# A two-layer decoder trunk on one core: POOL takes the candidate adds and half of the up stage's splits, the lookup goes by ranks, the row products read their common row in PSUM, ten chunks stand beside the search

## The chip, the core and the metric

The kernel runs on one core of a Trainium2 chip. A core has five engines that run their own instruction queues in order: TensorE (PE), VectorE (DVE), ScalarE (ACT), GpSimd (POOL) and SyncE (SP), which here only issues DMAs. They wait for each other through semaphores. The metric is the device time of one execution in microseconds.

## The reference

Two layers, each a mixer of three kinds of attention and then a PEER expert network; at the end a norm. The change touches the PEER part alone, for 512 tokens of width 1024:

```python
q = (xc @ w_q).reshape(PEER_CHUNK, PEER_HEADS, 2, PEER_DK_HALF)     # 8 heads, 2 x 128
s1 = jnp.einsum('thd,nd->thn', q[:, :, 0], k1f)                      # 128 sub-keys each
s2 = jnp.einsum('thd,nd->thn', q[:, :, 1], k2f)
v1, i1 = lax.top_k(s1, 16)
v2, i2 = lax.top_k(s2, 16)
cand = v1[..., :, None] + v2[..., None, :]                           # 16 x 16 pairs
cand_id = i1[..., :, None] * 128 + i2[..., None, :]
top_s, top_pos = lax.top_k(cand, 16)
ids = jnp.take_along_axis(cand_id, top_pos, axis=-1)
g = jax.nn.softmax(top_s, axis=-1)
act = jnp.einsum('thkd,td->thk', u[ids], xc)
w = g * jax.nn.gelu(act, approximate=False)
y = jnp.einsum('thk,thkd->td', w, v[ids])
```

u and v are tables of 16384 experts x 1024, float32.

## The kernel before

All weights come through one stream of chunks of 128 x 2048 float32 (1 MB), two slots deep. For each chunk SyncE loads `raw[s]`, ACT writes `hi[s]`, the chunk rounded to fp32r (`split_hi`, L501), and DVE or POOL writes `lo[s] = raw - hi` (`split_lo`, DVE L836, POOL L462). PE multiplies each pair by three matmuls (`product`, L1325 to L1327: hi x hi, lo x hi, hi x lo) and so keeps float32's precision. SyncE loads a slot again when `lo_done` says that it has been split.

The PEER part of a layer goes through these stages:

- Query stage, 8 chunks, one per head: queries, then the scores of its sub-keys; ACT puts these into `scores`.
- Search, on DVE, beside the query stage and the first chunks of the up stage. `top16` finds the best 16 of 128 keys for 4 token tiles x 2 halves (`vals`, `top_i`), two adds (L1106, L1108) form 112 candidate pairs per token (4 x 16 and 12 x 4), and a second `top16` finds the best 16 pairs. After eight heads comes the lookup: the place of each pair is taken apart into two ranks (L1117 to L1130), and for a = 1 to 15 one compare (L1150) marks where a rank is a and one predicated copy (L1153) puts the a-th key's number there, each over 1024 elements. Then the softmax is finished (L1161 to L1167), and `idx_t`, `g_t`, `ids` are ready.
- Up stage, 64 chunks: `experts` computes act for 352 tokens and all experts, 48 matmuls a chunk, in two halves i = 0 and 1 into banks 0 and 1; ACT evacuates them by gelu (L703, L706) and stores them to HBM. The first FIND_STEPS = 14 chunks run beside the search. Chunks 2 to 8 are split in halves by POOL (HALVED, L480), the next by DVE in between the lookup's operations, at a in LOW_HALF_AT.
- After chunk 13 PE transposes the indices and gates into banks 2 to 4 (L1611 to L1613). It waits there for `idx_done` and `g_done` of DVE. Then 30 gate steps follow, each with one chunk and three groups of four tokens, for which DVE and ACT make one-hots and PE multiplies them (L1623) into banks 4 to 7, which ACT evacuates (L749) to HBM. 20 chunks without groups follow: the tail.
- The other 160 (32 "extra" tokens, spread over partitions, and 128 of tile 3) go by gathered rows: POOL fetches 128 rows of u with one indirect DMA into one of NR = 7 slots (L490), DVE multiplies them by the token's row (`x_e` for the first 32 operations, L1202, `x_row` for the rest, L1204) and sums. 32 + 128 such products stand in the gate steps and the tail.
- Down stage, 64 chunks of v: gates and activations come back from HBM, are multiplied (L1238), split (L791, L1243), and `weighted` runs 48 matmuls per chunk into all eight banks in the order V_BLOCKS. The rows of v are fetched and accumulated beside it (L1212, L1215).

Every engine's order is written out by hand in the code. DVE and ACT split one chunk ahead of PE (`ahead`).

```python
for i in range(2):
    experts(st // 2, st % 2, i, halved=st if st in HALVED else None)
for tt in IDX_AT.get(st, ()):
    pe.wait_ge(idx_done, l * NT + tt + 1)
    pe.wait_ge(g_done, l + 1)
```

## Time and profile before

| | us |
|---|---|
| median of 3 runs | 3315.04 |
| lowest and highest | 3309.36, 3315.66 |
| the profiled execution | 3316.17 |
| its span, first to last instruction | 3314.4 |
| PE busy in the span | 3269.3 |
| DVE busy | 2610.5 |
| ACT busy | 1554.9 |
| POOL busy | 1087.6 |

The mean granted clock of TensorE is 0.998 of full speed. In the timelines a row is a start, a duration, the engine, the line of the kernel, the operation with its output and inputs, and in square brackets the engine's idle time before it and what ended that. Matmuls overlap, so their pace is read from start to start. In layer 0 the query stage begins at 484 us, the up stage at 586, the gate steps at 695, their last chunk ends at 1004, the down stage begins at 1158 and ends at 1650.

### The profile page before, as it was taken

What the parts mean: (1) busy time and instruction counts of PE and PEld (TensorE: products, weight loads), DVE (VectorE), ACT (ScalarE), POOL (GpSimd) and SP (SyncE); (2) the same over time, 40 slices, a digit from 0 to 9 for tenths busy, and PEclk for the clock granted to TensorE, in tenths of its full rate; (3) what the DMA queues carried; (4) which work ended last, traced back from release to release, by engine and by line L of the source; (5) the groups of instructions that cost most, each with busy time, mean ns of one, the idle gap of its engine ahead of it and who ended that gap; (6) DMA issues with size and microseconds to landing.
All of it is one profiled execution on the core that took longest, in us unless ns stands there. A gap on an engine that the chain in (4) does not pass through costs nothing. (4 is left out here: it accounts for less than half of the span.)

```text
span 3314.4 us, 55810 instructions
## 1 busy us (share of the span) xinstructions
PE 3269.3 (99%) x19734; PEld 3039.2 (92%) x19734; DVE 2610.5 (79%) x4992; ACT 1554.9 (47%) x2368; POOL 1087.6 (33%) x711
## 2 busy tenths in 40 slices
PE   8999999999999999999999999999999999999998
PEld 7767878999999999999987678789999999999998
DVE  6555448999997899999855644399999978999897
ACT  5554332467774333333355543334677733333333
POOL 1000003423335555555300000134333345555552
PEclk9999999999999999999999999999999999999999
DMA  4113322479999999999721133224899999999996
GB/s 146 62 52 115 140 104 81 171 286 383 379 383 389 420 403 411 403 409 410 284 90 64 42 124 140 103 82 176 310 379 382 378 404 416 402 409 407 404 405 251
DMA packets 230935, 894.83 MB, mean 270 GB/s; under 512 B 22784, under 2 KB 67984, under 8 KB 182912
## 3 DMA queue, kind: packets, MB, share of 16 engines
q1 hardware_dynamic: 116944, 465.34, 36.7%
q0 software_dynamic: 93008, 337.91, 26.1%
q10 hardware_dynamic: 20832, 89.74, 6.7%
q8 instruction: 72, 1.18, 0.1%
q14 instruction: 79, 0.65, 0.1%
HBM read 801.42 MB, written 91.49 MB: 269 GB/s over the span
## 5 line engine op out<-in xcount | busy, mean ns | idle before, releaser
L836 DVE TENSOR_TENSOR lo<-raw,hi 128x2048 fp32r<-128x2048 f32 (+1 forms) x320 | 728.9, 2278 | 287.4 <-ACT hi L501 284.9
L1325 PE MATMUL bank<-xT_hi,hi 128*128 128x352 f32 (+1 forms) x2688 | 928.7, 346 | 1.9 <-DVE xT_lo L886 1.7
L1326 PE MATMUL bank<-xT_lo,hi 128*128 128x352 f32 (+1 forms) x2688 | 911.5, 339 | 0.0
L1327 PE MATMUL bank<-xT_hi,lo 128*128 128x352 f32 (+1 forms) x2688 | 911.3, 339 | 0.0
L501 ACT ACTIVATE hi<-raw 128x2048 fp32r<-128x2048 f32 (+1 forms) x338 | 643.9, 1905 | 375.9 <-PE bank L1327 338.2
L1325 PE MATMUL bank<-w_hi,hi 128*128 128x352 f32 x2048 | 661.1, 323 | 0.5 <-DVE w_lo L1243 0.5
L1327 PE MATMUL bank<-w_hi,lo 128*128 128x352 f32 x2048 | 661.5, 323 | 0.0
L1326 PE MATMUL bank<-w_lo,hi 128*128 128x352 f32 x2048 | 658.1, 321 | 0.0
L1325 PEld LDWEIGHTS bank<-xT_hi,hi 128*128 128x128 f32 x2688 | 506.5, 188 | 32.3 <-issue 5.6
L490 POOL DMA_INDIRECT rows<-in_v_rows,ids x256 | 415.8, 1624 | 350.5 <-DVE h L1215 276.1
L1327 PEld LDWEIGHTS bank<-xT_hi,lo 128*128 128x128 f32 x2688 | 505.7, 188 | 26.0
L1326 PEld LDWEIGHTS bank<-xT_lo,hi 128*128 128x128 f32 x2688 | 507.2, 189 | 23.1
L490 POOL DMA_INDIRECT rows<-in_u_rows,ids x256 | 325.3, 1271 | 394.0 <-DVE act_row L1204 309.8
L1327 PEld LDWEIGHTS bank<-w_hi,lo 128*128 128x128 f32 x2048 | 386.7, 189 | 0.0
L1325 PEld LDWEIGHTS bank<-w_hi,hi 128*128 128x128 f32 x2048 | 384.4, 188 | 1.6 <-issue 1.0
L1326 PEld LDWEIGHTS bank<-w_lo,hi 128*128 128x128 f32 x2048 | 385.8, 188 | 0.0
L1215 DVE SCALAR_TENSOR_TENSOR h<-rows,w_row,h 128x1024 f32<-128x1024 f32 x256 | 327.6, 1280 | 7.3 <-DVE h L1215 1.4
L1204 DVE CUSTOM_DVE_ANT_0 rows<-rows,x_row 128x1024 f32<-128x1024 f32 x256 | 301.1, 1220 | 12.6 <-DMA rows<-in_u_rows,ids 12.6
L791 ACT ACTIVATE w_hi<-act_in 128x704 fp32r<-128x704 f32 x120 | 95.3, 794 | 392.2 <-DVE act_in L1238 392.2
L706 ACT ACTIVATE act_s<-bank 128x352 f32<-128x352 f32 x124 | 57.6, 465 | 278.3 <-PE bank L1327 278.3
L1262 DVE TENSOR_SCALAR onehot<-iota_sb,idx1T,gT 128x128 f32<-128x128 f32 x704 | 185.8, 356 | 1.0 <-ACT gT L738 1.0
L1623 PE MATMUL bank<-onehot 128*128 128x128 f32 x1408 | 176.0, 275 | 0.0
(227 smaller groups left out, 4254.1 us busy)
## 6 DMA issues: line engine op xcount, KB each, us to landing
raw<-in_stream SPq DMA_DIRECT2D x352, 1024.0 KB, 6.6
gate_d<-gate_s ACTq DMA_DIRECT2D x22, 2048.0 KB, 11.9
act_d<-act_s ACTq DMA_DIRECT2D x120, 352.0 KB, 6.4
act_in<-act_d SPq DMA_DIRECT2D x120, 352.0 KB, 7.0
gate_in<-gate_d SPq DMA_DIRECT2D x96, 384.0 KB, 9.6
gate_in<-gate_d SPq DMA_DIRECT2D x32, 256.0 KB, 4.8
rows<-in_u_rows,ids POOLq DMA_INDIRECT x256, 10.0
rows<-in_v_rows,ids POOLq DMA_INDIRECT x256, 7.5
```

Source lines behind the costliest of these rows:

```text
L490: pool.indirect_dma_start(rows[:, N % NR], None, a["u_rows" if n < U_ROW_OPS else "v_rows"], bass.IndirectOffsetOnAxis(which, 0)).then_inc ...
L501: act.activation(hi[s][:, 0:n], raw[s][:, 0:n], ACT.Copy).then_inc(hi_done, 1)
L706: act.activation(dst[:, s, 1, 0:TU], ps[1][:, 0:TU], ACT.Gelu).then_inc(gelu1, 1)
L791: act.activation(w_hi[:, s], acts_of(k, s), ACT.Copy).then_inc(w_hi_done, 1)
L836: dve.tensor_tensor(lo[s][:, 0:n], raw[s][:, 0:n], hi[s][:, 0:n].bitcast(F32), ALU.subtract).then_inc(lo_done, 1)
L1204: last = dve.tensor_tensor_reduce(row, row, x_row[:], 1.0, 0.0, ALU.mult, ALU.add, act_row[:, k])
L1215: last = dve.scalar_tensor_tensor(out=h[:, ROWED], in0=row, scalar=w_row[:, k], in1=h[:, ROWED], op0=ALU.mult, op1=ALU.add)
L1262: last = dve.tensor_scalar(o[:, r, 0], iota[:], idx1T[:, t], gT[:, t], ALU.is_equal, ALU.mult)
L1325: pe.matmul(dst, a_[0], b_[0], start=first, stop=False)
L1326: pe.matmul(dst, a_[0], b_[1], start=False, stop=False)
L1327: return pe.matmul(dst, a_[1], b_[0], start=False, stop=last)
L1623: last = pe.matmul(ps[4 + slot][:, tile(r)], o[:, 1], o[:, 0], start=True, stop=True)
```

## The change

Six edits belong together:

- POOL makes the candidate adds. DVE signals `vals_done` after each head's keys and works on the next head's keys before it takes the pairs of this one, after `cand_done`. `vals` and `cand` become double. POOL's adds stand in its queue behind the splits that CAND_AFTER names.
- The lookup goes by ranks. A head's 16 places are sorted, and the rank of the place k is at most k, so the compare for a runs over places a to 15 only, and so does the predicated copy. Their shapes become 64 x (16 - a) elements.
- FIND_STEPS is 10 instead of 14: the transposes of the indices stand behind chunk 9, the gate steps begin with chunk 10, and the tail has 24 chunks. Of DVE's splits within the lookup two are left, chunk 9 at a = 4 and chunk 10 at the end.
- From chunk 11 to 63 (SHARED) DVE makes the first half of `lo` and POOL the second (`second_half`), between its row fetches. PE waits for `lo0_done` before half i = 0 and for `lo_done` before i = 1.
- The row products read x_e and later x_row in banks 2 and 3 of PSUM (`x_in_ps`). ACT copies them there, x_e at gate step 0 after `e_link`, x_row at step E_GELU, now 10, after 32 row products. `rows_by` keeps the first 32 before that.
- V_BLOCKS starts with bank 4, and PE waits before bank 2 of the first chunk of the down stage until all 160 row products are done.

```diff
-FIND_STEPS = 14
-EXP_STEP, IDX_AT = 7, {13: (0, 1, 2)}
+FIND_STEPS = 10
+EXP_STEP, IDX_AT = 7, {9: (0, 1, 2)}
...
-V_BLOCKS = (2, 3, 4, 5, 6, 7, 0, 1)
+V_BLOCKS = (4, 5, 6, 7, 2, 3, 0, 1)
 ROW_PAIR = 2
-E_GELU, E_WEIGH = 12, 14
+E_GELU, E_WEIGH = 10, 12
...
-LOW_HALF_AT = (3, 5, 8, 10, 13)
+SHARED = range(FIND_STEPS + 1, C_U)
+LO0_PER_LAYER = len(HALVED) + len(SHARED)
...
+def rows_by(st):
+
+    if st >= G_STEPS:
+        return ROWS_IN_G + (st + 1 - G_STEPS) * (U_ROW_OPS - ROWS_IN_G) // TAIL_STEPS
+    n = st * ROWS_IN_G // (G_STEPS - 1)
+    return min(n, E) if st <= E_GELU else n
...
+LOW_HALF_AT = (4,)
+CAND_AFTER = {3: 0, 4: 1, 5: 2, 7: 3, 8: 4, 9: 5, 11: 6, 12: 7}
...
+                def candidates(hd):
+                    v, c = vals[:, hd % 2], cand[:, hd % 2]
+                    near, far = NEAR * TOPK, TOPK - NEAR
+                    pool.wait_ge(vals_done, PH * l + hd + 1)
+                    pool.tensor_tensor(c[:, :, 0:near].rearrange("p t (a b) -> p t a b", a=NEAR),
+                                       bc(v[:, :, 0, 0:NEAR], 3, TOPK), bc(v[:, :, 1], 2, NEAR), ALU.add)
+                    pool.tensor_tensor(c[:, :, near:].rearrange("p t (a b) -> p t a b", a=far),
+                                       bc(v[:, :, 0, NEAR:], 3, FAR), bc(v[:, :, 1, 0:FAR], 2, far),
+                                       ALU.add).then_inc(cand_done, 1)
+
+                for n in range(1, C_WQ + 2):
+                    split_lo(lp + P_WQ + n // 2, n % 2)
+                    if n in CAND_AFTER:
+                        candidates(CAND_AFTER[n])
...
+                    if C_WQ + c in CAND_AFTER:
+                        candidates(CAND_AFTER[C_WQ + c])
...
+                def second_half(c):
+                    s, half = c % 2, slice(HALF, CW)
+                    pool.wait_ge(lo0_done, LO0_PER_LAYER * l + len(HALVED) + c - FIND_STEPS)
+                    pool.tensor_tensor(lo[s][:, half], raw[s][:, half], hi[s][:, half].bitcast(F32),
+                                       ALU.subtract).then_inc(lo_done, 1)
+
+                for n in range(NR):
+                    fetch(n)
+                n = NR
+                for c in SHARED:
+                    second_half(c)
+                    while n < rows_by(c - SHARED.start) + NR:
+                        fetch(n)
+                        n += 1
...
+                    if st == 0:
+                        act.wait_ge(e_link, 5 * l + 5)
+                        act.activation(x_in_ps, x_e, ACT.Copy).then_inc(x_ps_set, 1)
                     if st == E_GELU:
                         act.wait_ge(row_done, ROW_OPS * l + E)
+                        act.activation(x_in_ps, x_row[:], ACT.Copy).then_inc(x_ps_set, 1)
                         act.activation(w_e[:], act_e[:], ACT.Gelu).then_inc(e_gelu, 1)
...
+                best_keys(0)
+                for hd in range(1, PH):
+                    best_keys(hd)
+                    best_pairs(hd - 1)
+                best_pairs(PH - 1)
...
-                        at[a] = looked(dve.tensor_scalar(chosen[a % 2], slot_f, float(a), None, ALU.is_equal))
+                        at[a] = looked(dve.tensor_scalar(by_rank(chosen[a % 2])[:, :, a:], by_rank(slot_f)[:, :, a:],
+                                                         float(a), None, ALU.is_equal))
...
-                        last = dve.tensor_tensor_reduce(row, row, x_e, 1.0, 0.0, ALU.mult, ALU.add, act_e[:, n:n + 1])
+                        last = dve.tensor_tensor_reduce(row, row, x_in_ps, 1.0, 0.0, ALU.mult, ALU.add, act_e[:, n:n + 1])
...
-                    ahead(p, s)
+                    c = FIND_STEPS + st + 1
+                    if c in SHARED:
+                        dve.wait_ge(hi_done, 2 * (lp + P_U) + c + 1)
+                        half = slice(0, HALF)
+                        dve.tensor_tensor(lo[c % 2][:, half], raw[c % 2][:, half], hi[c % 2][:, half].bitcast(F32),
+                                          ALU.subtract).then_inc(lo0_done, 1)
...
+                        elif shared and i == 0:
+                            pe.wait_ge(lo0_done, LO0_PER_LAYER * l + len(HALVED) + 2 * j + s - FIND_STEPS)
...
                     for x, d in enumerate(V_BLOCKS):
+                        if first and d == 2:
+                            pe.wait_ge(row_done, ROW_OPS * l + U_ROW_OPS)
```

What that does to the queues is shown at three places. First DVE at the end of the lookup, before. `rows` holds the compare's flags and the found numbers, `lo<-raw,hi` is a split, `g_sum` and `idx_t` belong to the results:

```order
L836 TENSOR_TENSOR lo<-raw,hi 128x2048
L1150 TENSOR_SCALAR rows<-rows 128x1024
L1153 COPY_PREDICATED rows<-rows,top_i 128x1024
L1150 TENSOR_SCALAR rows<-rows 128x1024
L1153 COPY_PREDICATED rows<-rows,top_i 128x1024 x2
L836 TENSOR_TENSOR lo<-raw,hi 128x2048
L1161 TENSOR_REDUCE g_sum<-g_t 128x32
L1163 RECIPROCAL g_sum<-g_sum 128x32
L1165 CAST idx_t<-rows 128x256 x4
L1167 TENSOR_TENSOR g_t<-g_t,g_sum 128x512
```

and with the change, from the split of chunk 9 and again at the end:

```order
L1217 COPY_PREDICATED rows<-rows,top_i 128x64x13
L891 TENSOR_TENSOR lo<-raw,hi 128x2048
L1213 TENSOR_SCALAR rows<-rows 128x64x11
L1217 COPY_PREDICATED rows<-rows,top_i 128x64x12
L1213 TENSOR_SCALAR rows<-rows 128x64x10
L1217 COPY_PREDICATED rows<-rows,top_i 128x64x11
...
L1217 COPY_PREDICATED rows<-rows,top_i 128x64x2
L1217 COPY_PREDICATED rows<-rows,top_i 128x64
L891 TENSOR_TENSOR lo<-raw,hi 128x2048
L1226 TENSOR_REDUCE g_sum<-g_t 128x32
```

One split stands at a = 4 and one behind the last copy; between them the shapes fall from 64 x 12 to 64 x 1.

Second, POOL from the last halves of the search to the first row fetches, before, and below it with the change:

```order
L480 TENSOR_TENSOR lo<-raw,hi 128x1024 x14
L490 DMA rows<-in_u_rows,ids_e 128x1024 x32
L490 DMA rows<-in_u_rows,ids 128x1024 x128
L490 DMA rows<-in_v_rows,ids_e 128x1024 x32
L490 DMA rows<-in_v_rows,ids 128x1024 x128
```

```order
L494 TENSOR_TENSOR cand<-vals 128x4x64
L496 TENSOR_TENSOR cand<-vals 128x4x48
L512 TENSOR_TENSOR lo<-raw,hi 128x1024 x8
L523 DMA rows<-in_u_rows,ids_e 128x1024 x7
L530 TENSOR_TENSOR lo<-raw,hi 128x1024 x2
L523 DMA rows<-in_u_rows,ids_e 128x1024 x3
L530 TENSOR_TENSOR lo<-raw,hi 128x1024
```

The second halves now stand between the fetches, and the first of them behind seven fetches.

Third, ACT at the first gate step, from its rounded copy of the next chunk, before and with the change:

```order
L501 ACTIVATE hi<-raw 128x2048
L761 ACTIVATE onehot<-iota_sb,idx2T 128x128 x4
L764 ACTIVATE onehot<-onehot,one 128x4x128
L703 ACTIVATE act_s<-bank 128x352
L706 ACTIVATE act_s<-bank 128x352
```

```order
L552 ACTIVATE hi<-raw 128x2048
L812 ACTIVATE onehot<-iota_sb,idx2T 128x128 x4
L815 ACTIVATE onehot<-onehot,one 128x4x128
L827 ACTIVATE bank_3<-rows 128x1024
L754 ACTIVATE act_s<-bank 128x352
L757 ACTIVATE act_s<-bank 128x352
```

The copy of x_e into PSUM stands in front of the two gelu evacuations of the chunk.

## Rows read from the trace of the kernel before

**Rows 1.** The page, busy time, share and instructions of each engine:

```profile
PE 3269.3 (99%) x19734; PEld 3039.2 (92%) x19734; DVE 2610.5 (79%) x4992; ACT 1554.9 (47%) x2368; POOL 1087.6 (33%) x711
```

**Rows 2.** Stretches of layer 0: span, busy by engine (instructions), clock, DMA share, GB/s.

```profile
586.00:694.00 108.00, 107.92 (x671) 107.61 (x669) 104.15 (x347) 44.61 (x54) 39.09 (x15) 1.00 0.48 173
695.00:1004.00 309.00, 309.00 (x2148) 309.00 (x2147) 290.65 (x616) 240.81 (x482) 121.72 (x101) 1.00 0.97 376
1004.00:1158.00 154.00, 153.96 (x964) 153.63 (x962) 119.07 (x145) 57.45 (x62) 90.10 (x64) 1.00 1.01 406
```

**Rows 3.** Timeline of PE where chunk 13 ends, in both layers.

```profile
693.94 0.32 PE L1327 MATMUL bank<-xT_hi,lo 128*128 128x352 f32 x1
694.29 0.30 PE L1611 MATMUL bank<-ident_sb,idx_t 128*128 128x128 f32 x1
...
2342.93 0.30 PE L1611 MATMUL bank<-ident_sb,idx_t 128*128 128x128 f32 x1
```

**Rows 4.** Timeline of VectorE in the lookup of layer 0.

```profile
637.18 0.41 DVE L1122 TENSOR_SCALAR left<-top_p 128x512 uint32<-128x512 uint32 x1
...
637.85 2.63 DVE L1124 TENSOR_SCALAR qhT<-top_p 128x512 uint32<-128x512 uint32 x1
...
641.40 0.76 DVE L1130 COPY_PREDICATED left<-qhT 128x512 uint32<-128x512 uint32 x1
...
650.81 2.29 DVE L836 TENSOR_TENSOR lo<-raw,hi 128x2048 fp32r<-128x2048 f32 x1 [0.50 <-ACT hi L501]
653.02 0.69 DVE L1150 TENSOR_SCALAR rows<-rows 128x1024 f32<-128x1024 f32 x1
653.62 1.38 DVE L1153 COPY_PREDICATED rows<-rows,top_i 128x1024 uint32<-128x1024 uint32 x1
655.03 0.70 DVE L1150 TENSOR_SCALAR rows<-rows 128x1024 f32<-128x1024 f32 x1
...
689.58 2.28 DVE L836 TENSOR_TENSOR lo<-raw,hi 128x2048 fp32r<-128x2048 f32 x1
```

**Rows 5.** Timelines of VectorE at two heads' beginnings, and of POOL.

```profile
523.51 1.63 DVE L1085 MAX8 vals<-rows 128x8 f32<-128x128 f32 x8
...
538.07 1.63 DVE L1085 MAX8 vals<-rows 128x8 f32<-128x128 f32 x8
...
637.79 2.40 POOL L480 TENSOR_TENSOR lo<-raw,hi 128x1024 fp32r<-128x1024 f32 x1 [1.15 <-ACT hi L721]
641.66 2.71 POOL L480 TENSOR_TENSOR lo<-raw,hi 128x1024 fp32r<-128x1024 f32 x1 [1.47 <-ACT hi L721]
```

**Rows 6.** Timeline of ACT: rounding chunk 9, and evacuating chunk 9.

```profile
648.86 1.92 ACT L501 ACTIVATE hi<-raw 128x2048 fp32r<-128x2048 f32 x1 [0.49 <-ACT act_s L706]
...
663.37 0.47 ACT L706 ACTIVATE act_s<-bank 128x352 f32<-128x352 f32 x1 [3.40 <-PE bank L1327]
```

**Rows 7.** Timelines of VectorE, PE and POOL in the first gate step.

```profile
702.25 2.13 DVE L1192 COPY rows<-rows 32x1024 f32<-32x1024 f32 x3
...
703.85 0.41 PE L1325 MATMUL bank<-xT_hi,hi 128*128 128x352 f32 x1
...
706.22 0.98 POOL L490 DMA_INDIRECT rows<-in_u_rows,ids_e  x1 [0.30 <-issue]
```

**Rows 8.** Timelines of PE and VectorE in one later gate step.

```profile
713.74 0.69 DVE L1258 TENSOR_TENSOR onehot<-iota_sb,idx2T 128x512 f32<-128x512 f32 x1
714.20 0.41 PE L1325 MATMUL bank<-xT_hi,hi 128*128 128x352 f32 x1
714.34 3.16 DVE L1262 TENSOR_SCALAR onehot<-iota_sb,idx1T,gT 128x128 f32<-128x128 f32 x12
...
719.62 1.22 DVE L1202 CUSTOM_DVE_ANT_0 rows<-rows 128x1024 f32<-128x1024 f32 x1
```

**Rows 9.** Timelines where the down stage begins: PE's first matmul, VectorE's last product.

```profile
1158.09 0.40 PE L1325 MATMUL bank<-w_hi,hi 128*128 128x352 f32 x1
...
1160.15 1.22 DVE L1204 CUSTOM_DVE_ANT_0 rows<-rows,x_row 128x1024 f32<-128x1024 f32 x1
```

More of the change, by code:

```diff
@@ L217, in sem, with bank @@
             return ctx.enter_context(nc.semaphore(name))
-        ps = [ctx.enter_context(nc.psum_tensor(f"bank{i}", [P, T], F32)) for i in range(8)]
+        def bank(i, shape):
+            return ctx.enter_context(nc.psum_tensor(f"bank{i}", shape, F32))
+        ps = [bank(i, [P, T]) for i in range(2)]
+        x_ps_row = bank("2_3", [P, 2, T])
+        ps += [x_ps_row[:, i] for i in range(2)]
+        ps += [bank(i, [P, T]) for i in range(4, 8)]
+        x_in_ps = x_ps_row[:].rearrange("p b t -> p (b t)")
         h = sb("h", [P, NT, D])
@@ L1587, in _, with experts @@
                 q_steps(PH // 2 - 1, True)
[L1589 removed]
+                def experts(j, s, i, first=0, end=NK, halved=None, shared=False):
                     k = l * C_U + 2 * j + s
```

60 lines of the change are left out of this document (33 added, 27 removed).

## The prediction

> **What bounds the kernel now.** I read the busy shares first, then the table of stretches, then the timelines of single engines around the place where the search hands its result to TensorE. PE is busy 3269.3 us of a span of 3314.4 us [rows 1]. The reader should see in the stretches that this is no average over good and bad stages: in layer 0 PE idles 0.08 us in the search part of the up stage, nothing in the gate part and 0.04 us in its tail, at full granted clock [rows 2]. The second layer runs the same schedule 1648.6 us later (694.29 and 2342.93) [rows 3]. VectorE is at 94% (290.65 of 309 us) in the gate part and POOL at 39%; both are spare engines, and work taken from them is worth only the PE idle time that they cause, 0.1 us per layer here. So the change can't make these stages shorter. It can only add idle time, if a result that PE waits for comes later against PE's own clockwork of chunks, or if PE meets it earlier.
>
> There is one such meeting that has no slack. Before, PE starts its last matmul of chunk 13 at 693.94 and the transposes of the found indices (L1611) at 694.29 [rows 3]. At the pace of a matmul, 0.16 us (964 of them in 154 us of the tail [rows 2]), it could have started at 694.10: it waits 0.2 us, VectorE came just in time. The change puts this meeting four chunks earlier. ACT begins to evacuate chunk 9 at 663.37 [rows 6], so PE is ready then at the latest, and VectorE has to be ready 31 us earlier than before.
>
> **The change part by part.**
>
> *Candidates on POOL.* VectorE's head takes 14.56 us (523.51 to 538.07) [rows 5], and the two adds are part of it. Taking the old head time for all as a bound, the search of eight heads ends by 523.51 + 7 x 14.56 = 625.4; that is on the safe side of a search without the adds. POOL's adds replace two VectorE instructions of 448 elements; at POOL's 2.4 us for 1024 elements [rows 5] that is 1.1 us, at most 3 with short runs. POOL waits for `vals_done` with the following splits queued behind. Those splits come 12.7 us apart in the query stage and 7.7 us apart after it, one chunk ahead of PE, and the waits I get for head 7, the tightest, are under 3 us. I take 0 for PE; the cover is that lead of a chunk.
>
> *The lookup, and what pins it.* After the search come 11.0 us of VectorE work to a = 4 (the shift, six index operations of about 0.33 us, two predicated copies, a cast, a copy, four compares, three predicated copies). POOL still splits until 641.66 + 2.7, and an operation of VectorE that meets it waits: the same 512-element operation took 0.41 us at 637.18 and 2.63 us at 637.85, next to POOL's 637.79 [rows 4, 5]. Five such halves cost 12 us: 625.4 + 11.0 + 12 = 648.4. So VectorE reaches the split of chunk 9, which the new list puts at a = 4, before 650.81, when ACT's rounded copy (648.86 + 1.92) allows it [rows 4, 6]. All that is saved in front of this point turns into waiting for ACT. What is left behind it decides.
>
> Behind it stand 11 compares and 12 predicated copies, then the split of chunk 10, then the sums. By shape the compares read 64 x (11 + ... + 1) = 4224 elements and the copies 64 x (12 + ... + 1) = 4992. A compare of 1024 advances VectorE 0.60 us (653.02 to 653.62), one of 512 0.33 us (0.41 less an overlap of about 0.08): 0.52 ns per element and 0.07 us each, so 2.2 + 0.8 = 3.0 us. A predicated copy lasts 1.38 us for 1024 and 0.76 for 512: 1.21 ns per element and 0.14 us, and the next compare waits for its end, 0.03 us more: 6.05 + 2.05 = 8.1 us [rows 4]. The split of chunk 9 is over when the next compare begins, at 653.0 as before; the lookup ends at 653.0 + 11.1 = 664.1; the split of chunk 10 and the way to the first transpose take what they took before, 694.29 - 689.58 = 4.7 us [rows 3, 4]. PE starts the transposes at 668.8 instead of 663.4: 5.4 us of idle time, **10.8 us for both layers**. Nothing gives it back, since PE has no gaps later on that could shrink. Lower bound: only the elements count, 2.2 + 6.05 = 8.25 us, 2.6 of idle time per layer. Upper bound: an operation under 512 elements is no cheaper than one of 512 (8 compares and 8 copies are under it): 4.0 + 10.3 = 14.3 us, 8.6 per layer.
>
> A rule of the Trainium skill bears on the compares ("VectorE: DVE Perf Modes", section "What auto-detection actually checks"): an fp32 operation with one source keeps its double rate if the outermost dimension is even. Here it is 64, so the cut should not halve the rate; if it did, 2.2 us per layer would come on top. The 0.52 ns per element of the rows is half of what the predicated copies show per element, and no row has a cut shape.
>
> *ACT fills PSUM at step 0.* ACT now waits for `e_link` and copies x_e before its gelu of chunk 10, which stands behind it in its queue, and PE needs that gelu for chunk 11. In the times of before: the three copies of L1192 end at 702.25 + 2.13 = 704.4, 1.15 us earlier with half a split in front, 703.2; a copy of 2048 elements on ACT is 1.92 us, so one of 1024 about 1.0, and the gelu is 0.47; so 704.7 against 703.85, when PE starts the next chunk [rows 6, 7]. With the handing over that is 1.0 us per layer, **2.0 in all**, between 0 and 3 each. POOL's first second half stands behind seven row fetches (the last ends at 706.22 + 0.98, some 1 us less now), ends near 708.7, and PE wants it half a chunk after 703.85 + 1.0, with the first gate group about 709.5; no cost. The load of chunk 13 goes out 8 us later than before, after that half, and is inside the range.
>
> *Shared splits from chunk 11.* VectorE loses 1.1 us per step, POOL gets 2.4. A gate step is 714.20 - 703.85 = 10.35 us. VectorE needs 0.6 + 3.1 + 1.1 + 3.3 x 1.15 = 8.6 us, POOL 2.4 + 3.3 x 1.3 = 6.7 [rows 7, 8]. Both fit, the half is done 5 us before PE asks, so 0. SyncE's reload of `raw` waits for the later half, 1.3 us, against a lead of one and a half steps: 0. The gelu of the extra tokens, now at step 10, waits there for row 31. The products of a step begin 719.62 - 714.20 = 5.4 us into it, 4.3 with half a split in front, and three of them end at 7.8; a copy of 1.0, a small gelu of some 0.3 and the chunk's gelu of 0.5 make it 9.6 of 10.35 [rows 8]: 0.
>
> *PSUM banks 2 and 3 at the start of the down stage.* PE now waits for all 160 row products before the fifth block, 24 matmuls or 3.8 us after 1158.09. The last product began at 1160.15 and took 1.2 us, and now fewer stand in the last step [rows 9]: 0.
>
> **Sum.** 3316.17 of the profiled execution (its span of 3314.4 and 1.8 around it) + 10.8 + 2.0 = 3329.0. The median of the runs shown is 1.1 us below that execution, so I forecast **3328 us**, 0.4% slower. A measurement of this kernel can tell about 0.2% (6.6 us) from no change.
>
> **The rivals.**
>
> *Late lookup*, as worked out, or somewhat shorter or longer: 3322 to 3338. Chance 0.63.
>
> *The lookup costs by its elements alone* (the side on which it is not slower). The fixed part of the short operations hides under their neighbours and ACT's extra copy slips under PE's chunk: 2.6 per layer, 3320 us. It decides below 9.0 us for the 23 operations, from where the sum stays under 0.2%. For it: a copy starts before the compare ahead of it has ended (653.62 against 653.02 + 0.69). Against it: each compare waits for the copy ahead of it (655.03 after 653.62 + 1.38) [rows 4]. Chance 0.17.
>
> *POOL's halves hold up VectorE's row products.* The operation at 637.85 shows that an operation can be held for POOL's whole 2.4 us [rows 4, 5]. If reading x from PSUM does not free the product of this, VectorE needs 8.6 + 2.4 = 11.0 us per gate step against 10.35, 30 steps per layer: 0.65 x 60 = 39 us, 3367. It decides above 1.8 us of hold per step. Chance 0.06. The Trainium skill ("SBUF — State Buffer", section "SBUF: two separate sides") says that GpSimd excludes those VectorE operations that have two SBUF inputs or use two ports; by that rule the product, with one input in PSUM, is free and this rival falls. The held row agrees with the rule; no row of before has a product with a PSUM input beside a POOL operation.
>
> *POOL is the bound in the tail.* With a second half of 2.4 us and 2.67 fetches of 2.2 us each, were they that slow, POOL would need 8.3 us against 7.7 us of a chunk; over 23 steps its lead of 5 us is used up and about 8 us per layer are lost: 3344. It decides above 2.0 us per fetch; the row shows 1.3 with the pause in front of it [rows 7]. Chance 0.06.
>
> *Faster than before by over 0.2%.* The idle time to be won in these stages is 0.2 us; this needs a shift of the pace itself. Chance 0.04. The remaining 0.04 is no visible stall at all.
>
> **How the numbers follow.** Over 0.2% slower: 0.63 + 0.06 + 0.06 = 0.75; within 0.2%: 0.17 + 0.04 = 0.21; faster 0.04. The bounds 2 x 2.6 and 2 x (8.6 + 3) on 3315 give 3320 to 3338; taking in part of the POOL rival at the top and the spread of the runs at the bottom, the range is 3317 to 3342.
>
> **What would show it.** PE idle 5 to 6 us before the transposes, released by VectorE; VectorE idle before its split of chunk 9, released by ACT; its last predicated copy about 11 us behind that split; about 1 us PE idle at the first gelu of chunk 11, released by ACT; nothing at the down stage. Wrong: no PE idle at the transposes, or row products over 1.3 us beside POOL's halves, or VectorE already late at the split of chunk 9.

## The result

The changed kernel takes 3329.2 us (median of 5 runs, 3326.9 to 3332.1) against 3315.0 of the kernel before: ratio 1.0048, 95% interval 1.0033 to 1.0062. It is 0.5% slower. The profiled execution took 3330.4 us, its span is 3328.6.

Busy times on the page of the changed kernel; [rows 1] is that of before:

```profile
PE 3271.3 (98%) x19734; PEld 3042.9 (91%) x19734; DVE 2461.0 (74%) x4960; ACT 1558.5 (47%) x2372; POOL 1256.3 (38%) x849
```

VectorE gave up 150 us of work and the kernel became slower. TensorE's busy time grew by 2 us, its idle time by 12. The stretches of layer 0 (columns as in [rows 2]) show where:

```profile
586.00:694.00 108.00, 101.50 (x632) 100.96 (x631) 101.17 (x374) 50.50 (x80) 57.06 (x33) 0.97 0.52 184
695.00:1004.00 309.00, 309.00 (x2138) 309.00 (x2137) 249.95 (x583) 234.64 (x458) 165.49 (x128) 1.00 0.97 379
1004.00:1158.00 154.00, 154.00 (x964) 154.00 (x963) 87.22 (x130) 56.44 (x60) 101.39 (x74) 1.00 1.00 381
```

The gate part and the tail are as full as before. The first stretch has 6.5 us of idle time that [rows 2] doesn't have, and its mean clock is 0.97. The timeline of PE at the transposes, both layers, answers to [rows 3]:

```profile
664.38 0.32 PE L1402 MATMUL bank<-xT_hi,lo 128*128 128x352 f32 x1
671.12 0.45 PE L1688 MATMUL bank<-ident_sb,idx_t 128*128 128x128 f32 x1 [6.42 <-DVE idx_t L1230]
...
2315.48 0.32 PE L1402 MATMUL bank<-xT_hi,lo 128*128 128x352 f32 x1
2322.18 0.45 PE L1688 MATMUL bank<-ident_sb,idx_t 128*128 128x128 f32 x1 [6.39 <-DVE idx_t L1230]
```

TensorE waits 6.4 us for VectorE in each layer. Short windows of layer 0 from the beginning of that wait on (the number before the last two is the granted clock):

```profile
664.00:668.00 4.00, 0.70 (x5) 0.41 (x3) 3.86 (x9) 0.46 (x1) 0.00 (x0) 1.00 0.00 0
668.00:671.00 3.00, 0.00 (x0) 0.00 (x0) 2.97 (x9) 0.00 (x0) 0.00 (x0) 0.65 0.30 66
671.00:672.00 1.00, 0.88 (x4) 0.91 (x5) 0.94 (x7) 0.00 (x0) 0.00 (x0) 0.50 1.02 434
...
674.00:675.00 1.00, 1.00 (x5) 1.00 (x4) 0.87 (x4) 0.90 (x1) 0.92 (x1) 0.50 0.76 301
675.00:676.00 1.00, 1.00 (x6) 1.00 (x5) 0.33 (x2) 1.00 (x2) 0.78 (x1) 0.64 0.72 141
676.00:678.00 2.00, 2.00 (x15) 2.00 (x14) 1.92 (x2) 1.91 (x6) 1.70 (x2) 1.00 0.86 289
```

The granted clock falls from 1.00 to 0.50 (1.2 GHz) during the idle time and is back at 1.00 (2.4 GHz) only at about 675.7, 4.6 us after the first transpose. In layer 1 it is back 5.6 us after it. The count of matmuls in a window of 1 us (those that overlap its edges included) is 4 to 6 until then, and 15 in 2 us afterwards. This was in no part of the forecast.

The timeline of VectorE, in place of [rows 4]: the end of the search, POOL's halves holding single operations, the split of chunk 9, the rest of the lookup:

```profile
626.08 0.69 DVE L1178 TENSOR_TENSOR g_t<-top_s 128x512 f32<-128x512 f32 x1
...
639.20 3.61 DVE L1217 COPY_PREDICATED rows<-rows,top_i 128x960 uint32<-128x960 uint32 x1
...
643.36 3.54 DVE L1217 COPY_PREDICATED rows<-rows,top_i 128x896 uint32<-128x896 uint32 x1
...
647.40 1.32 DVE L1217 COPY_PREDICATED rows<-rows,top_i 128x832 uint32<-128x832 uint32 x1
652.17 2.29 DVE L891 TENSOR_TENSOR lo<-raw,hi 128x2048 fp32r<-128x2048 f32 x1 [3.45 <-ACT hi L552]
654.38 0.52 DVE L1213 TENSOR_SCALAR rows<-rows 128x704 f32<-128x704 f32 x1
654.82 1.03 DVE L1217 COPY_PREDICATED rows<-rows,top_i 128x768 uint32<-128x768 uint32 x1
...
656.29 1.07 DVE L1217 COPY_PREDICATED rows<-rows,top_i 128x704 uint32<-128x704 uint32 x1
...
659.20 1.03 DVE L1217 COPY_PREDICATED rows<-rows,top_i 128x576 uint32<-128x576 uint32 x1
...
660.57 0.71 DVE L1217 COPY_PREDICATED rows<-rows,top_i 128x512 uint32<-128x512 uint32 x1
...
665.66 0.92 DVE L1217 COPY_PREDICATED rows<-rows,top_i 128x128 uint32<-128x128 uint32 x2
666.33 2.37 DVE L891 TENSOR_TENSOR lo<-raw,hi 128x2048 fp32r<-128x2048 f32 x1
```

VectorE stands 3.45 us in front of its split of chunk 9 until ACT's rounded copy is there, then needs 11.95 us for the rest of the lookup (654.38 to 666.33), 2.3 for the split of chunk 10 and 2.5 for sums and casts.

For the accounting I read the length of each stage from the starts of PE's matmuls (us). The third line, from the first gate matmul to the first one of the last group, is called the gate part from here on:

| | before, layers 0, 1 | changed, layers 0, 1 |
|---|---|---|
| idle time at the transposes beyond a matmul's pace | 0.2, 0.2 | 6.6, 6.5 |
| first transpose to first gate matmul | 8.7, 8.7 | 10.9, 11.3 |
| first gate matmul to the first of the last group | 299.4, 299.4 | 299.4, 299.4 |
| up stage as a whole | 572.6, 572.3 | 580.6, 581.0 |
| down stage | 492.0, 492.9 | 488.1, 494.5 |

The up stage is 8.0 and 8.8 us longer: 6.4 and 6.3 us of idle time, 2.1 and 2.6 us of half clock (the second line), less 0.5 and 0.2 of small changes. That is 16.8 us; the spans of the two profiled executions differ by 14.2, and so do the medians. Between the spans, 2.3 us are in the down stages, whose length varies by itself (last experiment), and 0.3 us are in the rest. The rest holds half-clock stretches of 3.4 us that both kernels have outside the PEER part and that don't come in every execution. One of them stands in the profile of before behind this wait of PE, at the end of layer 0 (the window is the one behind the row):

```profile
1658.42 1.08 PE L1350 MATMUL bank<-ident_sb,xs 128*128 128x128 f32 x6 [2.21 <-DVE xs L875]
1659.00:1662.00 3.00, 3.00 (x16) 3.00 (x15) 1.07 (x3) 0.60 (x3) 0.00 (x0) 0.50 0.00 0
```

In the changed kernel's profile the wait at this place is 2.39 us, and the clock stays at 1.00.

### The profile page after: what moved, and what is told of

Read it like the earlier page. It is cut to its first block, busy times and chain, and to the rows that moved or that the text cites. A ratio compares the mean times of both kernels' runs of the same rounds, so it can differ in the third digit from the quotient of the medians.

```text
span 3328.6 us, 56198 instructions
## 1 busy us (share of the span) xinstructions
PE 3271.3 (98%) x19734; PEld 3042.9 (91%) x19734; DVE 2461.0 (74%) x4960; ACT 1558.5 (47%) x2372; POOL 1256.3 (38%) x849
## 4 chain that ended last, share of the span: by engine, by line
PE 95%; DVE 2%; ACT 1%; issue 1%; DMA 0%; SPq 0%; DVEq 0%; ACTq 0%
PE bank L1400 29%; PE bank L1402 28%; PE bank L1401 28%; PE bank L1700 5%; PE bank L1515 1%; PE bank L1530 1%; PE bank L1549 1%; PE bank L1648 1%; DVE rows L1217 0%; DMA raw<-in_stream 0%; PE bank L1497 0%; PE bank L1520 0%; DVE lo L891 0%; DVE lg L1032 0%; DVE rows L1213 0%
## 5 line engine op out<-in xcount | busy, mean ns | idle before, releaser
L891 DVE TENSOR_TENSOR lo<-raw,hi 128x2048 fp32r<-128x2048 f32 (+1 forms) x214 | 486.5, 2273 | 203.2 <-ACT hi L552 200.2
L530 POOL TENSOR_TENSOR lo<-raw,hi 128x1024 fp32r<-128x1024 f32 x106 | 255.0, 2405 | 319.4 <-DVE lo L1335 319.3
L1335 DVE TENSOR_TENSOR lo<-raw,hi 128x1024 fp32r<-128x1024 f32 x106 | 130.0, 1226 | 253.7 <-ACT hi L552 253.7
L1271 DVE CUSTOM_DVE_ANT_0 rows<-rows,bank 128x1024 f32<-128x1024 f32 x256 | 298.7, 1216 | 0.0
L523 POOL DMA_INDIRECT rows<-in_u_rows,ids x256 | 244.4, 955 | 68.3 <-issue 60.3
```

The costliest lines, as they stand in the source:

```text
L523: pool.indirect_dma_start(rows[:, N % NR], None, a["u_rows" if n < U_ROW_OPS else "v_rows"], bass.IndirectOffsetOnAxis(which, 0)).then_inc ...
L530: pool.tensor_tensor(lo[s][:, half], raw[s][:, half], hi[s][:, half].bitcast(F32), ALU.subtract).then_inc(lo_done, 1)
L891: dve.tensor_tensor(lo[s][:, 0:n], raw[s][:, 0:n], hi[s][:, 0:n].bitcast(F32), ALU.subtract).then_inc(lo_done, 1)
L1271: last = dve.tensor_tensor_reduce(row, row, x_in_ps, 1.0, 0.0, ALU.mult, ALU.add, act_row[:, k])
L1335: dve.tensor_tensor(lo[c % 2][:, half], raw[c % 2][:, half], hi[c % 2][:, half].bitcast(F32), ALU.subtract).then_inc(lo0_done, 1)
```

## The experiments

My theory after this: everything that the change costs is made at the transposes, by idle time that VectorE's order of work causes and by the half clock that follows. The main rival: one of the other edits costs something by itself.

### Twelve chunks beside the search

```diff
-FIND_STEPS = 10
-EXP_STEP, IDX_AT = 7, {9: (0, 1, 2)}
+FIND_STEPS = 12
+EXP_STEP, IDX_AT = 7, {11: (0, 1, 2)}
...
-LOW_HALF_AT = (4,)
+LOW_HALF_AT = (4, 8, 12)
```

> The changed kernel with the transposes behind chunk 11 instead of chunk 9 (FIND_STEPS 12), with splits of chunks 9, 10, 11 inside the lookup and of 12 at its end; every other edit stays. Theory (the whole loss is made at the transposes: TensorE waits for the lookup there and then runs at half clock for some us): TensorE is ready 15.45 us later, VectorE only by two more splits and ACT's copy of chunk 12; idle before the transposes 0 to 1 us instead of 6.6, no stretch at granted clock 0.50, time 3313 to 3317, that is the 3315 of the kernel before. Rival (POOL's second halves, the copies into PSUM, the new block order or the candidates on POOL cost something by themselves): it stays at 3320 or above although the idle time is gone.

Measured: 3313.1 us against 3313.2 of the kernel before, ratio 0.9998 (0.9989 to 1.0007). Idle time 0.1 us in both layers. Timeline of PE, the first transpose and the one place with idle time behind it:

```profile
678.86 0.30 PE L1688 MATMUL bank<-ident_sb,idx_t 128*128 128x128 f32 x1
...
689.38 0.43 PE L1400 MATMUL bank<-xT_hi,hi 128*128 128x352 f32 x1 [0.77 <-ACT act_s L754]
```

All other edits are in this kernel, and in sum it costs nothing against the kernel before. The rival falls, with one exception that the second row shows: the gap released by ACT's gelu, in both layers, and a gate part of 300.4 us instead of 299.4. That is the forecast's term for ACT's copy into PSUM. In the changed kernel it isn't there:

```profile
680.78 1.03 ACT L827 ACTIVATE bank<-rows 128x1024 f32<-128x1024 f32 x1 [2.84 <-DVE rows L1257]
681.75 0.45 ACT L754 ACTIVATE act_s<-bank 128x352 f32<-128x352 f32 x1
```

The gelu ends at 682.2, and TensorE, slowed by the half clock, arrives for it at 682.81.

### Keeping TensorE busy while it waits

```diff
+                    if st == FIND_STEPS - 1:
+                        pe.wait_ge(g_ev, l * GROUPS + G_RING)
+                        for n in range(40):
+                            pe.matmul(ps[4][:, 0:TU], xT_hi[:, n % NK, 0:P], xT_hi[:, n % NK, 0:TU], start=True, stop=True)
                     for tt in IDX_AT.get(st, ()):
```

> The changed kernel, and TensorE runs 40 matmuls of 352 columns into the free bank 4, whose result nobody reads, between its last matmul of chunk 9 and its wait for the indices: 40 x 0.16 = 6.4 us of work in the 6.6 us of idle time. Theory (the idle time is followed by a stretch at half clock, which costs about 2.1 us per layer on top): the transposes start as late as before, 6.6 us behind chunk 9, but the granted clock stays at 1.00, the three groups of transposes take 0.9 us instead of 1.8 and the first gate chunk's matmuls 0.16 instead of 0.29; time 3329 less 2 x 2.1 = 3325. Rival (the slow stretch has another cause, such as the kind of instruction or DMA traffic there): the clock falls to 0.50 again and the time stays at 3329.

Measured: 3327.7 us (3325.5 to 3332.7). The windows at the same place:

```profile
668.00:671.00 3.00, 2.94 (x21) 2.68 (x21) 2.90 (x13) 0.30 (x2) 0.00 (x0) 1.00 0.64 208
671.00:672.00 1.00, 1.00 (x9) 1.00 (x8) 0.94 (x7) 1.00 (x8) 0.00 (x0) 1.00 0.99 418
```

The clock stays at 1.00, from the first transpose to the first gate matmul it is 8.7 us again in both layers, and the idle time is what triggers the half clock. The gain is smaller than expected, 1.0 and 1.8 us of up stage per layer: with TensorE at full clock the gap of 0.8 us for ACT's gelu appears (gate part 300.4 us in both). The median, 3325 by the expectation, differs from the changed kernel's by less than the spread of the runs; the mechanism rests on the clock and the stage lengths.

### The split of chunk 9 later in the lookup

```diff
-LOW_HALF_AT = (4,)
+LOW_HALF_AT = (7,)
```

> The changed kernel with the split of chunk 9 at a = 7 instead of a = 4, nothing else. Theory (VectorE waits 3.45 us for ACT's copy of chunk 9 and only what stands behind the split counts): the wait goes, three pairs of compare and copy (4.7 us) move in front of the split, which starts up to 1.3 us later than at 652.2 and still ends before TensorE wants chunk 9 at 656.7; idle before the transposes 6.5 - 3.4 = 3.1 us per layer, 3329 - 6.8 = 3322, and 3318 if the clock stays at 1.00 behind so short an idle time. Rival (TensorE's idle time is set by VectorE's load as a whole, by POOL's halves that hold it): the transposes stay where they are, 3329.

Measured: 3320.2 us (3315.1 to 3326.5), idle 3.1 us in both layers. VectorE no longer waits for ACT. What stands behind the split counts, not the load as a whole. The windows over the transposes in layer 0 and in layer 1:

```profile
666.00:667.00 1.00, 0.87 (x8) 0.90 (x9) 0.94 (x7) 0.31 (x2) 0.00 (x0) 1.00 1.02 434
...
2321.00:2322.00 1.00, 1.00 (x6) 1.00 (x7) 0.96 (x7) 0.19 (x2) 0.00 (x0) 0.50 0.95 401
```

The same 3.1 us of idle time left the clock alone in one layer and halved it in the other. In the 12 layers of the profiles with 6.5 us or more at this place it fell each time. The runs give no length below which it is safe: the next variant has a half-clock stretch after waits of 3.5 us in both gate parts and one after 2.3 us where the second down stage begins.

### Row products from SBUF

```diff
-                        last = dve.tensor_tensor_reduce(row, row, x_in_ps, 1.0, 0.0, ALU.mult, ALU.add, act_e[:, n:n + 1])
+                        last = dve.tensor_tensor_reduce(row, row, x_e, 1.0, 0.0, ALU.mult, ALU.add, act_e[:, n:n + 1])
...
-                        last = dve.tensor_tensor_reduce(row, row, x_in_ps, 1.0, 0.0, ALU.mult, ALU.add, act_row[:, k])
+                        last = dve.tensor_tensor_reduce(row, row, x_row[:], 1.0, 0.0, ALU.mult, ALU.add, act_row[:, k])
```

> The changed kernel, but the row products read x_e and x_row from SBUF as the kernel before did; ACT still makes its copies into PSUM, and POOL its second halves. Theory (a VectorE operation with both inputs in SBUF is held while a POOL operation runs, one with an input in PSUM is not): products that meet a second half take up to 1.2 + 2.4 us; VectorE needs 8.1 us per gate step now (250 us busy in 309) and up to 10.5 then, against 10.3: the mean product rises from 1.22 to 1.7 us or more, and the time to between 3329 (all held time fits into VectorE's idle time) and 3350. Rival (the products are never held, wherever x stands): a mean of 1.22 us and 3329.

Measured: 3362.7 us, ratio to before 1.0147 (1.0132 to 1.0163). In order: the group of products in the changed kernel; the same group here; one product and the half of POOL beside it in the changed kernel; one held product and the half beside it here.

```profile
L1271 DVE CUSTOM_DVE_ANT_0 rows<-rows,bank 128x1024 f32<-128x1024 f32 x124 | 144.6, 1216 | 0.0
```

```profile
L1271 DVE CUSTOM_DVE_ANT_0 rows<-rows,x_row 128x1024 f32<-128x1024 f32 x126 | 215.7, 1757 | 2.7 <-DMA rows<-in_u_rows,ids 2.7
```

```profile
689.57 1.21 DVE L1269 CUSTOM_DVE_ANT_0 rows<-rows,bank 128x1024 f32<-128x1024 f32 x1
688.59 2.41 POOL L530 TENSOR_TENSOR lo<-raw,hi 128x1024 fp32r<-128x1024 f32 x1 [2.59 <-DVE lo L1335]
```

```profile
741.76 3.38 DVE L1269 CUSTOM_DVE_ANT_0 rows<-rows 128x1024 f32<-128x1024 f32 x1
```

```profile
740.78 3.28 POOL L530 TENSOR_TENSOR lo<-raw,hi 128x1024 fp32r<-128x1024 f32 x1 [2.20 <-DVE lo L1335]
```

With both inputs in SBUF a product is held until POOL's operation ends, 3.38 us instead of 1.2. POOL is held in turn: its half lasts 3.28 us here instead of 2.41, and a fetch of a u row 1.46 us on average instead of 0.96. The gate part grows to 311.3 and 312.3 us, the up stage as a whole to 596.5 and 599.8, together 34.6 us more than in the changed kernel. The time lies above the 3350 us that the expectation allowed; the expectation counted VectorE's time in a gate step and neither POOL's delay nor the tail. So the copies into PSUM are what makes POOL's second halves possible without a loss, and the mechanism of the forecast's rival of 39 us is real for this variant, by 33.5 us. The trace agrees with the Trainium skill's rule that the forecast cites ("SBUF — State Buffer", section "SBUF: two separate sides"), for two inputs in SBUF and for one in PSUM.

### POOL splits two chunks less beside the lookup

```diff
-HALVED = range(2, 9)
+HALVED = range(2, 7)
...
-LOW_HALF_AT = (4,)
+LOW_HALF_AT = (2, 5, 9)
```

> The changed kernel with its 10 chunks beside the search, but POOL makes the halves of chunks 2 to 6 only; VectorE splits 7, 8, 9 inside the lookup (at a = 2, 5, 9) and 10 at its end. Theory (each POOL half holds a VectorE operation of the lookup by about 2.2 us, so a chunk in POOL's hands costs VectorE 4.4 us there, against 2.3 us if it splits it itself, and splits in its order fill the wait for ACT): five held operations become one, idle before the transposes falls from 6.5 to about 1.3 us per layer, the clock stays at 1.00, the gap of 0.7 us at the second gate chunk appears; 3329 - 2 x (5.2 + 2.1) + 2 x 1.1 = 3316.6. Rival (work given back to VectorE in its busiest place makes the lookup later, as its share of busy time suggests): idle 6.5 + 2 x 2.3 = 11 us, 3338.

Measured: 3312.5 us, ratio to before 0.9989 (0.9980 to 0.9998). Idle time 0.1 us in both layers, with 10 chunks as in the changed kernel. VectorE's splits of chunks 7 to 10 and PE's first transpose:

```profile
635.30 2.29 DVE L891 TENSOR_TENSOR lo<-raw,hi 128x2048 fp32r<-128x2048 f32 x1 [0.16 <-ACT hi L552]
...
642.97 2.29 DVE L891 TENSOR_TENSOR lo<-raw,hi 128x2048 fp32r<-128x2048 f32 x1 [0.31 <-ACT hi L552]
...
650.67 2.29 DVE L891 TENSOR_TENSOR lo<-raw,hi 128x2048 fp32r<-128x2048 f32 x1
...
658.34 2.29 DVE L891 TENSOR_TENSOR lo<-raw,hi 128x2048 fp32r<-128x2048 f32 x1
```

```profile
663.06 0.30 PE L1688 MATMUL bank<-ident_sb,idx_t 128*128 128x128 f32 x1
```

VectorE got two splits more, 4.6 us, and is ready 6.9 us earlier (it casts the indices at 661.5 instead of 669.6, in a layer that began 1.1 us earlier). Four held operations are gone, about 2.2 us each, and of 3.45 us of waiting for ACT 0.5 are left. That is better than the expectation of 3316.6 with 1.3 us of idle time. Work that POOL takes from VectorE costs VectorE more, in this place, than doing it.

### The candidates back on VectorE

```diff
-                    dve.sem_inc(vals_done, 1)
...
+                    dve.tensor_tensor(c[:, :, 0:near].rearrange("p t (a b) -> p t a b", a=NEAR),
+                                      bc(v[:, :, 0, 0:NEAR], 3, TOPK), bc(v[:, :, 1], 2, NEAR), ALU.add)
...
+                                      ALU.add).then_inc(cand_done, 1)
```

POOL's two calls of `candidates` are taken out.

> The changed kernel with the candidate adds back on VectorE (the order of keys and pairs stays as changed), POOL without them. The search then ends some 9 us later, as in the kernel before. Theory (what is won ahead of the split of chunk 9 is lost to waiting for ACT and to POOL's halves, which hold VectorE's lookup operations but not its searches): of 9 us, 3.5 go into the wait for ACT and 4.4 into two halves that no longer meet the lookup; the split of chunk 9 starts about 1.2 us later, idle 7.7 us per layer, 3331 to 3332. Rival (the candidates on POOL are what makes 10 chunks possible at all, the full 9 us arrive at the transposes): 3347.

Measured: 3335.6 us (3330.1 to 3337.7), between the two. Idle time at the transposes 8.7 us, and 0.8 us before chunk 9. The search ends 13 us later, not 9, because the adds are held too:

```profile
L1159 DVE TENSOR_TENSOR cand<-vals 128x256 f32<-128x256 f32 x8 | 10.9, 1368 | 0.3
...
L1161 DVE TENSOR_TENSOR cand<-vals 128x192 f32<-128x192 f32 x8 | 5.0, 624 | 0.0
```

An unheld pair takes 0.42 + 0.35 us; eight take 15.9. Of the 13 us, 2.1 reach the transposes and 0.8 chunk 9; three halves fewer meet the lookup, and VectorE doesn't wait for ACT. The theory's mechanism stands, its size was short by 1.8 us per layer. The up stages are 2.2 and 2.0 us longer than the changed kernel's, which is 4.2 of the 6.4 us between the medians.

### The whole lookup

```diff
-                        at[a] = looked(dve.tensor_scalar(by_rank(chosen[a % 2])[:, :, a:], by_rank(slot_f)[:, :, a:],
-                                                         float(a), None, ALU.is_equal))
+                        at[a] = looked(dve.tensor_scalar(chosen[a % 2], slot_f, float(a), None, ALU.is_equal))
...
-                                                                bc(of_rank[:, :, a - 1], 2, TOPK - a + 1)))
+                                                                bc(of_place[:, :, :, a - 1], 3, TOPK)))
```

> The changed kernel with the lookup's compares and predicated copies over all 1024 elements again. Behind the split of chunk 9 stand 11 compares of 0.60 us advance and 12 copies of 1.40 us instead of 12.0 us in all: 23.4 us. Theory (only what stands behind that split counts, at full weight): idle 6.5 + 11.5 = 18 us per layer, 3329 + 23 = 3352 if the stretch at half clock behind the idle time stays as long as it is (about 4.7 us, 2.1 us lost); a longer one shows if the clock's price grows with the idle time. Rival (something later, such as the tail's reserve on VectorE or POOL, takes up part of it): under 3348.

Measured: 3346.2 us (3344.6 to 3351.1), idle 17.5 and 17.6 us:

```profile
680.75 0.45 PE L1686 MATMUL bank<-ident_sb,idx_t 128*128 128x128 f32 x1 [17.34 <-DVE idx_t L1228]
```

The up stage is 11.2 and 10.7 us longer than the changed kernel's, so what stands behind the split arrives nearly in full (11.5 expected). The median lies 6 us under the expectation, and also under the 3348 that the rival had named. The profile says why: both down stages are 488.1 us long, 6.4 us less than the two of the changed kernel's profile. The half-clock stretch costs 2.2 us after 17.5 us of idle time, about what it costs after 6.6.

### Lookup shapes in fours

```diff
-                        at[a] = looked(dve.tensor_scalar(by_rank(chosen[a % 2])[:, :, a:], by_rank(slot_f)[:, :, a:],
+                        at[a] = looked(dve.tensor_scalar(by_rank(chosen[a % 2])[:, :, a // 4 * 4:], by_rank(slot_f)[:, :, a // 4 * 4:],
```

The copy is cut in the same way.

> The changed kernel, but the compare and the copy for a run over places from a rounded down to a multiple of four (64 x 16, 12, 8 and 4 elements instead of 64 x (16 - a)); the superfluous places hold no such rank. Theory (a predicated copy takes its time in steps of 256 elements, 0.43, 0.71, 1.03, 1.35 us, as the changed kernel's rows show for 192 to 256, 320 to 512, 576 to 768, 832 to 1024): the copies of 64 x 8 take 0.71 us and those of 64 x 12 1.03 as before although they cover more elements; behind the split of chunk 9 only the compares (and the copies of 576 and 320, no longer a step apart) change, and the transposes come 0.5 to 1.0 us later, 3330 to 3331. Rival (duration goes by the element, 1.21 ns, as the forecast's sum took it): 64 x 18 more elements in copies and as many in compares behind the split: 1152 x (1.21 + 0.52) = 2.0 us per layer, 3333.

Measured: idle 7.2 and 7.3 us, 0.6 and 0.7 more than in the changed kernel; 3327.7 us (3323.6 to 3333.0), not told apart from it. This is the theory's 0.5 to 1.0 us and not the rival's 2.0. Copies by shape:

```profile
L1217 DVE COPY_PREDICATED rows<-rows,top_i 128x768 uint32<-128x768 uint32 x4 | 4.1, 1035 | 0.0
L1217 DVE COPY_PREDICATED rows<-rows,top_i 128x512 uint32<-128x512 uint32 x4 | 2.8, 708 | 0.0
...
L1217 DVE COPY_PREDICATED rows<-rows,top_i 128x256 uint32<-128x256 uint32 x4 | 1.8, 438 | 0.0
```

The steps hold. A copy of 768 lasts 1.03 us, as those of 704 (1.07) and 576 (1.03) do in the changed kernel, and one of 512 takes the 0.71 of its 512.

### No second halves on POOL

```diff
-SHARED = range(FIND_STEPS + 1, C_U)
+SHARED = range(0)
```

with the waits that belong to it; VectorE makes the whole split in every step.

> The changed kernel without the second halves on POOL: VectorE makes the whole of every split from chunk 11 on, as in the kernel before; the row products still read PSUM. Theory (VectorE has room: 250 us busy in the 309 us of the gate part, 1.1 us more in each of 30 steps makes 283, under the 290.65 of the kernel before, and TensorE waits for nothing there): 3329, the same idle time at the transposes, the gate part at 299.4 us. Rival (the second halves win or cost something by themselves): the gate part or the tail of the up stage changes its length by over 0.5 us, or the fetches get shorter or longer and shift the down stage.

Measured: 3332.0 us (3330.4 to 3337.6), up stage 581.2 and 580.8 us against 580.6 and 581.0. TensorE is as full from 695 us on as with POOL's help, while VectorE is busy 282 us of 309:

```profile
695.00:1004.00 309.00, 309.00 (x2138) 309.00 (x2137) 282.16 (x580) 233.74 (x457) 92.56 (x98) 1.00 0.97 379
```

The halves win and cost nothing in the up stage. In layer 0 the gate part is 300.6 us, with a gap of 1.0 us released by ACT's gelu; the half clock lasts 3.0 us behind the first transpose there, and not 4.6. The profiled execution is 7.2 us longer than the changed kernel's, and 7.0 of that are its two down stages of 494.9 us, the long length; for the 2.8 us between the medians that is likely, but not shown.

### ACT's copy elsewhere

First on the kernel of twelve chunks, with the copy at the end of gate step 0, behind both gelus:

```diff
-                    if st == 0:
-                        act.wait_ge(e_link, 5 * l + 5)
-                        act.activation(x_in_ps, x_e, ACT.Copy).then_inc(x_ps_set, 1)
...
                             store_gates(q // PER_SLICE)
+                    if st == 0:
+                        act.wait_ge(e_link, 5 * l + 5)
+                        act.activation(x_in_ps, x_e, ACT.Copy).then_inc(x_ps_set, 1)
```

> The kernel of e1_steps12, and ACT copies x_e into PSUM at the end of gate step 0 instead of before that step's gelu evacuations. e1 showed TensorE idle 0.70 us before the second gate chunk of each layer, released by that gelu, and a gate part 1.07 us longer than in the changed kernel (300.43 against 299.36 us). Theory (the copy in front of the gelu costs this, as the forecast's term of 1.0 us says; in the changed kernel the half clock of the first gate chunk hides it): the idle time of 0.70 us goes in both layers, the gate part is 299.4 again, and the time is e1's 3313.1 less 2.1 = 3311.0, some 0.06% under the kernel before. Rival (the gap comes from the evacuation's other inputs, or the first row product now waits for the copy and passes the wait on): the gap stays or moves to gate step 1, 3313 to 3315.

Measured: 3310.8 us, ratio to before 0.9992 (0.9983 to 1.0001). In layer 0 the gap is gone (gate part 299.7). In layer 1 it moved to the next step, 0.6 us (300.4), as the rival said. Then on e6_pool_to_6, between the two gelus:

```diff
-                    if st == 0:
-                        act.wait_ge(e_link, 5 * l + 5)
-                        act.activation(x_in_ps, x_e, ACT.Copy).then_inc(x_ps_set, 1)
...
                             gelu(j, s, b)
+                        if st == b == 0:
+                            act.wait_ge(e_link, 5 * l + 5)
+                            act.activation(x_in_ps, x_e, ACT.Copy).then_inc(x_ps_set, 1)
```

> The kernel of e6_pool_to_6 (10 chunks beside the search, no idle time at the transposes), and ACT copies x_e into PSUM between the two gelu evacuations of gate step 0, where it waits 3.3 us for TensorE, instead of in front of both. Theory (the copy in front costs 1.1 us per layer, seen in e6 as 0.72 us of idle time before the second gate chunk and a gate part of 300.5 us): the gap goes in both layers, the gate part is 299.4 us, and the time is 3312.5 - 2.1 = 3310.4, some 0.13% under the kernel before. Rival (as in the second layer of e5, where a copy behind both gelus made the next group of gates 0.62 us late: ACT has no room for the copy anywhere in that step): a gap of 0.6 us elsewhere, 3312.

```profile
670.58 0.44 ACT L754 ACTIVATE act_s<-bank 128x352 f32<-128x352 f32 x1
673.52 1.03 ACT L835 ACTIVATE bank<-rows 128x1024 f32<-128x1024 f32 x1 [2.50 <-DVE rows L1257]
674.49 0.45 ACT L757 ACTIVATE act_s<-bank 128x352 f32<-128x352 f32 x1
```

Measured: 3310.0 us (3305.7 to 3316.3), ratio to before 0.9989 (0.9980 to 0.9998). Both gate parts are 299.4 us, the up stages 572.1 and 571.6. It is the fastest kernel of the study by its median, 0.1% under the kernel before, where the changed one is 0.5% above it. That it beats e6 isn't shown by the times (the intervals are the same), only by the stage lengths.

### The kernel before once more

> The kernel before once more, for another profiled execution. In the eight kernels run so far the down stage of a layer took 488.1 to 488.8, 491.1 to 492.7 or 494.5 to 494.9 us, with TensorE busy throughout, whatever was changed ahead of it; in the profile of the kernel before 492.0 and 492.9. Theory (TensorE's pace in that stage takes one of a few values by chance, which makes most of the spread between runs): up stage, from its first matmul to the down stage, 572.3 to 572.6 us as before, in both layers, and down stages of about 488, 491.5 or 494.7 us. Rival (the new order of the banks made the down stage shorter): 492 to 493 in both layers again.

Measured: 3313.7 us in one run, up stage 572.3 us in both layers, down stages 488.8 and 494.1. So these lengths come without the new order of banks; that rival falls. One small difference is left: in both profiles of the kernel before, PE's second chunk of the down stage starts 0.4 to 0.5 us late, behind a wait for VectorE's `w_lo` (L1243), and with the change it doesn't. Which of the six edits does that isn't shown. In the changed kernel's trace TensorE is busy without a gap in both of its down stages, and still one lasts 488.1 and the other 494.5 us. With 64 chunks of 48 matmuls that is 0.1589 and 0.1610 us per matmul, both at clock 1.00. There the pace is the same from the first chunk of a stage to its last. What sets it stays open.

## Why the prediction was right, and where it was not

The forecast was 3328 us, "a late lookup", and 3329.2 came. The mechanism is the one that was forecast, and the number is closer than the terms behind it. Point by point:

- *TensorE ready at 663.4*: 663.2, from the profile after (664.38 + 0.16, less 1.4 us by which its layer starts later). *VectorE pinned by ACT's copy of chunk 9*: right; it waits 3.45 us, as the step said that all savings ahead turn into waiting. The experiments with chunk 9 later and with the candidates show it from both sides.
- *11.1 us behind the split*: 11.95. The compares were right (3.0 us). The copies took 8.9 instead of 8.1, since their time goes in steps of 256 elements and isn't the 1.21 ns per element plus 0.14 us of the sum. The cut compare of 64 x 8 elements took 0.43 us and an uncut operation of 512 takes 0.41, so the trace agrees with the rule of the Trainium skill that the forecast cites ("VectorE: DVE Perf Modes", section "What auto-detection actually checks"). *The way to the transposes, 4.7*: 4.8. Together the idle time is 6.6 us instead of 5.4; 6.4 and 6.3 of it are new, 12.7 in all instead of 10.8. A slip without consequence: in the upper bound 7 compares and 7 copies are under 512 elements, the eighth of each has 512 and the same price.
- *Missing: the clock.* The forecast took "full clock" from [rows 2] as given, though that clock stood beside a TensorE that never paused. The idle time halves it for the first 4.6 and 5.6 us of work behind it. That costs 2.1 and 2.6 us.
- *ACT's copy, 2.0 in all*: right as a mechanism, 1.0 to 1.1 us per layer of longer gate part where the clock is full at that place (e1, e2, e6, layer 0 of e3), and 0 in the changed kernel, because the half clock hides it. Two errors of opposite sign, 4.7 missing and 2.0 too many.
- *Candidates, second halves, banks 2 and 3: 0*: right, as far as e1 (all together) and e11 (the halves alone) show. POOL's halves hold VectorE's lookup as counted, five times.
- *Sum*: 12.8 forecast, 16.8 in the stages, 14.2 in the medians. By the stages the forecast was 4 us short. That 3328 lies so near to 3329.2 is in part luck: the missing clock and the surplus copy partly cancel, and 2.6 us are what else varies between runs.

The rival by elements alone fails on the steps. The rival of POOL's lock fails for products with an input in PSUM and is confirmed without it. POOL as the bound in the tail fails: its fetches of u rows take 0.96 us on average and not over 2.0. What no rival said is that the ten chunks fit: e6_pool_to_6 has no idle time with them, by another split of the same work.

## What to carry to other kernels

Where an engine hands over a result that another waits for, find the last thing in its queue that can't start earlier (here a split that waits for ACT) and count only what stands behind it. Before moving work from VectorE to POOL, look at which operations run beside it: a half of 2.4 us on POOL held VectorE for 2.2, nearly the whole 2.3 of the full split. A new idle time on TensorE of some microseconds is to be priced with a half-clock stretch behind it, here 1.4 to 2.8 us more, and gaps that this stretch hides come back when it is mended.

## What the runs showed of the hardware

- TensorE's granted clock fell to 0.50 in every layer with 6.5 to 17.6 us of idle time at the transposes, and in one of two with 3.1 us. It cost 1.4 to 2.8 us each time and didn't grow with the idle time. With 40 matmuls in place of the idle time it stayed at 1.00. Elsewhere it fell after waits of 3.5 us (twice, e4_x_in_sbuf) and of 2.3 us (once), and at the end of layer 0 after 2.21 us in one profile and not after 2.39 us in another. The gaps of 0.7 to 1.0 us behind the first gate chunk left it alone.
- A predicated copy of 4-byte elements took 0.44, 0.71, 1.03 and 1.38 us for 256, 512, 768 and 1024 elements per partition, and nearly the same within each step (0.44 us also for 64, 1.07 for 704, 1.31 for 832). The compare in front of it goes smoothly with size (0.22 us for 64, 0.43 for 512, 0.52 for 704).
- A VectorE product with two inputs in SBUF was held for the rest of a POOL half's time (3.38 instead of 1.2 us), with one input in PSUM not (1.21 us beside a half of 2.41). The lookup's compares, index operations and predicated copies were held too (3.61 instead of 1.38 us for a copy of 960), and `top16`'s operations (MAX8, FIND_INDEX8, MATCH_REPLACE8) were not: 0.26 to 0.29 us with POOL's half beside them or without.
- The same down stage, TensorE full and at clock 1.00, lasted 488 to 489, 491 to 493 or 494 to 495 us, differently in two layers of one execution. It makes steps of about 3.4 us in a kernel's time.
